# State-space heads computed with channels in the partitions instead of positions

## The reference, cut to what matters

```python
xbc = silu(causal_dwconv(xbc, conv_w, conv_b)); xs, bm, cm = split(xbc)
a_cs = cumsum(dt * a)                                   # per head
lmat = exp(where(causal, a_cs[l] - a_cs[s], -inf))      # decays between positions
y_diag = (cm @ bm.T * lmat) @ (xs * dt)                 # inside a chunk, per head
y_off  = (cm @ prev_state) * exp(a_cs)                  # what the first chunk leaves to the second
y = y_diag + y_off + xs * d_skip
out = rmsnorm(y * silu(z)) * norm_g                     # z = h @ w_in[:, 0:1024]
```

## Time and profile before

| | us |
|---|---|
| median of 3 runs | 2436.69 (2436.45 to 2437.45) |
| the profiled execution's own time | 2437.16 |
| its span in the profile | 2435.3 |
| PE busy | 2427.0 |
| PEld busy | 2022.1 |
| DVE busy | 1965.2 |
| ACT busy | 1263.7 |
| POOL busy | 106.7 |

### The profile page before, as it was taken

The page is one execution under the profiler, slowest core; times in us unless marked ns, Lnnn a source line. Parts: engine busy times, 40 slices in busy tenths (PEclk is TensorE's granted clock), DMA queues, the critical chain, the costliest instruction groups (busy, mean ns, idle before and its releaser), DMA issues.

```text
span 2435.3 us, 30633 instructions
## 1 busy us (share of the span) xinstructions
PE 2427.0 (100%) x11686; PEld 2022.1 (83%) x11686; DVE 1965.2 (81%) x3206; ACT 1263.7 (52%) x1680; POOL 106.7 (4%) x128
## 2 busy tenths in 40 slices
PE   9999999999999999999999999999999999999999
PEld 7888888888888888888888888888888888888887
DVE  8787978888888788888767798878878867797877
ACT  5445654454456544544556655544544557664543
POOL 0000000000000000000100020000000100020000
PEclk9999999999999999999999999999999999999999
DMA  8775455656754566676564564565666644555663
GB/s 259 236 242 169 158 188 192 193 186 196 238 179 156 176 197 197 205 231 209 176 197 139 175 215 156 191 196 181 209 193 201 200 162 153 173 203 167 200 194 122
DMA packets 325905, 463.35 MB, mean 190 GB/s; under 512 B 18608, under 2 KB 237056, under 8 KB 325504
## 3 DMA queue, kind: packets, MB, share of 16 engines
q1 hardware_dynamic: 321792, 452.90, 57.3%
q10 hardware_dynamic: 3968, 8.49, 1.2%
HBM read 457.11 MB, written 4.23 MB: 189 GB/s over the span
## 4 chain that ended last, share of the span: by engine, by line
PE 98%; DVE 1%; DMA 1%; SPq 0%; ACT 0%; issue 0%; DVEq 0%; ACTq 0%
PE acc L733 47%; PE work L733 38%; PE acc L947 4%; PE acc L950 2%; PE work L1002 1%; PE acc L1039 1%; DMA raw<-ffn_w_dram 1%; PE work L740 1%; PE work L1020 1%; PE work L768 1%; DVE w_lo L1860 0%; PE acc L1280 0%; PE work L1190 0%; PE acc L1279 0%; PE acc L768 0%; PE work L1076 0%
## 5 line engine op out<-in xcount | busy, mean ns | idle before, releaser
L1860 DVE TENSOR_TENSOR w_lo<-raw,w_hi 128x2048 fp32r<-128x2048 f32 x416 | 947.7, 2283 | 214.3 <-ACT w_hi L1327 210.9
L1327 ACT CAST w_hi<-raw 128x2048 fp32r<-128x2048 f32 x416 | 789.2, 1903 | 292.1 <-PE acc L733 93.1
L733 PE MATMUL work<-w_hi,xt_both 128*128 128x512 f32 x2784 | 872.6, 389 | 0.8 <-DVE field L1964 0.8
L733 PEld LDWEIGHTS work<-w_hi,xt_both 128*128 128x128 f32 x2784 | 522.6, 188 | 110.5 <-issue 1.6
L733 PE MATMUL work<-w_lo,xt_both 128*128 128x512 f32 x1392 | 541.6, 389 | 0.0
L733 PE MATMUL acc<-w_hi,yt_hi 128*128 128x512 f32 x1088 | 427.1, 393 | 0.0
L733 PE MATMUL acc<-w_hi,yt_lo 128*128 128x512 f32 x1088 | 423.8, 389 | 0.0
L733 PE MATMUL acc<-w_lo,yt_hi 128*128 128x512 f32 x1088 | 423.4, 389 | 0.0
L2037 DVE STREAM_TRANSPOSE field<-field 32x128 f32<-32x128 f32 x1280 | 387.7, 303 | 19.1
L733 PE MATMUL acc<-w_hi,xt_both 128*128 128x512 f32 (+2 forms) x1280 | 393.9, 384 | 0.0
L733 PEld LDWEIGHTS work<-w_lo,xt_both 128*128 128x128 f32 x1392 | 261.3, 188 | 54.0
(11 more groups left out here) (210 smaller groups left out, 1600.7 us busy)
## 6 DMA issues: line engine op xcount, KB each, us to landing
raw<-ffn_w_dram SPq DMA_DIRECT2D x260, 512.0 KB, 4.6
raw<-w_in_dram SPq DMA_DIRECT2D x208, 512.0 KB, 4.5
raw<-w_ffn_in_dram SPq DMA_DIRECT2D x176, 512.0 KB, 4.7
raw<-w_ffn_out_dram SPq DMA_DIRECT2D x88, 512.0 KB, 4.3
raw<-w_branch_dram SPq DMA_DIRECT2D x48, 512.0 KB, 4.5
raw<-w_out_dram SPq DMA_DIRECT2D x32, 512.0 KB, 4.3
bias<-b_gate_dram SPq DMA_DIRECT2D x10, 512.0 KB, 5.6
raw<-w_branch_pool_dram SPq DMA_DIRECT2D x8, 512.0 KB, 4.3
```

What stands on the lines that cost most here:

```text
L733: last = nc.tensor.matmul(out, x[:, kt, k], y, start=start and n == 0, stop=stop and n == 2)
L1327: nc.scalar.copy(w_hi[:, slot, 0:n], raw[:, at, 0:n]).then_inc(hi_split[slot], 1)
L1860: nc.vector.tensor_tensor(w_lo[:, at, 0:n], raw[:, at, 0:n], w_hi[:, slot, 0:n].bitcast(F32), ALU.subtract).then_inc(unit_split[slot], 1)
```

## The change

- z is projected turned (`z_turned`): a 128x128 block of weight is stationary and 256 positions move, 192 matmuls in place of 96. DVE scales the result by the row factor as it reads it (`z_scaled`), ACT takes the silu in place (`z_silu`). The four z units are loaded as 256 columns by 8 row tiles instead of 512 by 4.
- The heads are computed turned, in four batches of four: a 128x64 block of `xdt` (or of `scaled`, what the first chunk carries over) is stationary, the masked decays (128 positions) move, two heads go to the two column halves of the array. The carried part is a third product per head that accumulates in PSUM, so `carried`, `carry` and the middle block's separate decay go. The decays after the first chunk are kept in two versions, `after` and the new `late`; POOL makes them with 32 instructions of 128x128.
- The skip part is one DVE instruction per 128x256 tile with d_skip per partition; the second product of `rows_xs` goes.
- The gated result is already turned: the 16 transposes go, ACT and DVE split it from SBUF. For the norm the sum runs over partitions: ACT squares, POOL adds the eight tiles (1024, 512 and 256 columns), PE multiplies by a column of -1 (`sqs`), DVE scales.
- `spread_sums(3)` is issued one z step earlier.

```diff
@@ SP
-                chunks("w_in_2", 0, 2)
+                for c in range(4):
+                    load(next(at), whole("w_in_2", l, 0, 256 * c, 256, 8))
@@ POOL
-                                nc.gpsimd.tensor_tensor(after[:, hd, :, :], after[:, hd, :, :],
-                                                        starts[:, :, hd:hd + 1].broadcast_to([P, 2, P]), ALU.subtract) \
+                                nc.gpsimd.tensor_tensor(after[:, hd, 0, :], after[:, hd, 0, :],
+                                                        starts[:, 0, hd:hd + 1].broadcast_to([P, P]), ALU.subtract) \
                                     .then_inc(after_ready, 1)
+                            pool.wait_ge(conv_ready, 3 * l + 3)
+                            for hd in range(16):
+                                nc.gpsimd.tensor_tensor(S["late"][:, hd, :], after[:, hd, 1, :],
+                                                        starts[:, 1, hd:hd + 1].broadcast_to([P, P]), ALU.subtract) \
+                                    .then_inc(late_ready, 1)
+                            pool.wait_ge(y_squared, 4 * l + 4)
+                            for k, n in enumerate((4, 2, 1)):
...
+                                nc.gpsimd.tensor_tensor(S["squares"][:, 0:n, :], S["squares"][:, 0:n, :],
+                                                        S["squares"][:, n:2 * n, :], ALU.add).then_inc(y_summed, 1)
@@ PE
-                chunk("z", 0, 40)
+                def z_turned(c, q):
...
+                    for j in range(2):
+                        out = acc[2 * pair + q][:, j * 256:(j + 1) * 256]
+                        for kt in range(kd):
...
+                            nc.tensor.matmul(out, hi, xt_hi[:, kt, :], start=kt == 0, stop=False)
+                            nc.tensor.matmul(out, hi, xt_lo[:, kt, :], start=False, stop=False)
+                            last = nc.tensor.matmul(out, lo, xt_hi[:, kt, :], start=False, stop=kt == kd - 1)
-                    nc.tensor.matmul(acc[2 * pair][:, c:c + 64], w[:, 0:P], S["xdt"][:, 0, v], start=True, stop=True)
-                    nc.tensor.matmul(acc[2 * pair + 1][:, c:c + 64], w[:, P:2 * P], S["xdt"][:, 1, v], start=True,
-                                     stop=True).then_inc(y_done, 1)
+                def heads(i):
+                    g = i // 2
+                    pair, n = count("chunks", 1, l, "ys", g)
+                    pe.wait_ge(chunk_read[pair], n * 2 - 1 + i % 2)
+                    pe.wait_ge(scaled_ready, 2 * l + g + 1)
+                    pe.wait_ge(seg_ready, 4 * l + i + 1)
+                    for t in range(2):
...
+                        for s in range(2):
+                            nc.tensor.matmul(out[s][:, early], S["xdt"][:, 0, v[s]], after[:, hds[s], 0, :],
+                                             start=True, stop=True)
+                        for s in range(2):
+                            nc.tensor.matmul(out[s][:, late], S["scaled"][g][:, hds[s] % 8 * 64:hds[s] % 8 * 64 + 64],
+                                             after[:, hds[s], 1, :], start=True, stop=False)
+                        for s in range(2):
+                            last = nc.tensor.matmul(out[s][:, late], S["xdt"][:, 1, v[s]], S["late"][:, hds[s], :],
+                                                    start=False, stop=True)
+                    last.then_inc(y_done, 1)
                 half("gate_s", 0, 0, 44, 0)
                 half("gate_s", 0, 0, 44, 1)
-                carried()
-                heads(range(0, 3))
+                heads(0)
                 half("gate_s", 0, 1, 44, 0)
-                heads(range(3, 6))
+                heads(1)
                 half("gate_s", 0, 1, 44, 1)
-                heads(range(6, 8))
                 half("gate_s", 1, 0, 46, 0)
-                heads(range(8, 11))
+                heads(2)
                 half("gate_s", 1, 0, 46, 1)
-                heads(range(11, 16))
+                heads(3)
                 half("gate_s", 1, 1, 46, 0)
-                turn(1, l, "turn_s", S["y"], range(4), lambda i: pe.wait_ge(y_ready, 2 * l + (1 + i // 2)))
                 half("gate_s", 1, 1, 46, 1)
-                chunk("br_s", 0, 48, yt, "turn_s")
+                both("br_s", 0, 0, 48, yt, "y")
+                both("br_s", 0, 1, 48, yt, "y")
+                bank, filled = fill(1, l, "sqs")
+                pe.wait_ge(y_summed, 3 * l + 3)
+                for r in range(2):
+                    last = nc.tensor.matmul(bank[:, r:r + 1], S["squares"][:, 0, r * P:(r + 1) * P], minus_one[:, 0:1],
+                                            start=True, stop=True)
@@ ACT: through(45) / z_silu(0, 0), z_silu(0, 1) / through(46) / z_silu(1, 0), z_silu(1, 1) / factors
+                def decays(i):
+                    hds = slice(BATCH * i, BATCH * (i + 1))
...
+                    nc.scalar.activation(x, x, ACT.Relu, scale=-1.0)
+                    nc.scalar.activation(y, y, ACT.Relu, scale=-1.0).then_inc(exponents_bounded, 1)
+                    act.wait_ge(exponents_bounded, 4 * l + i + 1)
+                    nc.scalar.activation(x, x, ACT.Exp, scale=-1.0)
+                    nc.scalar.activation(y, y, ACT.Exp, scale=-1.0).then_inc(decay_ready, 1)
                 decays(0)
                 through(47)
                 decays(1)
                 decays(2)
                 through(48)
                 decays(3)
-                decays(4)
@@ DVE, around rows_xs and the heads
+                z_scaled(1, 0)
                 through(45)
+                z_scaled(1, 1)
                 rows_xs(1)
...
+                def weights(i):
+                    dve.wait_ge(decay_ready, 4 * l + i + 1)
+                    x = after[:, BATCH * i:BATCH * (i + 1), :, :].rearrange("p h r q -> p h (r q)")
+                    tt(x, x, S["cb"][:, i // 2, 0:2 * P].unsqueeze(1).broadcast_to([P, BATCH, 2 * P]), ALU.mult)
+                    x = S["late"][:, BATCH * i:BATCH * (i + 1), :]
+                    tt(x, x, S["cb"][:, i // 2, 2 * P:3 * P].unsqueeze(1).broadcast_to([P, BATCH, P]), ALU.mult) \
+                        .then_inc(seg_ready, 1)
+                def outputs(i):
...
+                    for t in range(2):
+                        y = S["y"][:, 2 * i + t, :]
+                        last = stt(y, y, vec[:, 100 + 2 * i + t:101 + 2 * i + t],
+                                   acc[2 * pair + i % 2][:, t * 256:(t + 1) * 256], ALU.mult, ALU.add)
+                    last.then_inc(chunk_read[pair], 1)
...
+                    tt(y, y, S["z"][:, 2 * i:2 * i + 2, :], ALU.mult).then_inc(y_ready, 1)
+                scale_early(0)
+                weights(0)
                 through(47)
+                weights(1)
+                scale_early(1)
                 through(48)
                 add_bias(1, l, "gate_s", 0, m + 45, S["gate"][:, :, 0:512], 0, 0, (0,))
+                weights(2)
                 add_bias(1, l, "gate_s", 0, m + 45, S["gate"][:, :, 0:512], 0, 0, (1,))
+                outputs(0)
+                outputs(1)
+                weights(3)
                 through(49)
+                outputs(2)
+                outputs(3)
                 through(50)
+                for i in range(4):
+                    dve.wait_ge(y_hi, 4 * l + i + 1)
...
+                        last = stt(yt_lo[:, t, :], S["y"][:, t, :], vec[:, gain("s") + t:gain("s") + t + 1],
+                                   yt_hi[:, t, :].bitcast(F32), ALU.mult, ALU.subtract)
+                    last.then_inc(y_split, 1)
```

More of the change, by code:

```diff
@@ L104, in tables @@
         norms=Table(1, [norms]),
-        squares=Table(1, [[u for u in norms if not u[0][2].startswith("post_")]]),
+        squares=Table(1, [[u for u in norms if u[0][2].startswith("pre_") or u[0][2] == "final"]]),
         means=Table(1, [[u for u in norms if not u[0][2].startswith("pre_")]]),
@@ L932, in part @@
                     if turn_name and r == 0 and kt % 2 == 0:
-                        turned(block, l, turn_name, kt // 2)
+                        if name == "br_s":
+                            pe.wait_ge(y_split, 4 * l + kt // 2 + 1)
+                        else:
+                            turned(block, l, turn_name, kt // 2)
                     last = product(x[0], x[1], kt, r, pos, t * cols, cols, acc[2 * pair + r][:, 0:cols],
@@ L1283, in heads @@
-                def heads(hds):
-                    for hd in hds:
-                        weigh(hd)
+                def heads(i):
[5 more added lines that the diff above has]
+                    for t in range(2):
+                        hds = [BATCH * i + 2 * t + s for s in range(2)]
+                        early, late = (slice(t * 256 + r * P, t * 256 + (r + 1) * P) for r in range(2))
+                        out = [acc[2 * pair + i % 2][64 * s:64 * s + 64, :] for s in range(2)]
+                        v = [slice(hd * 64, hd * 64 + 64) for hd in hds]
+                        for s in range(2):
[8 more added lines that the diff above has]
```

(58 more changed lines are left out.)

119 lines of the change are left out of this document (66 added, 53 removed).

## The result

The changed kernel takes 2443.4 us (2443.18 to 2444.47, 8 runs) against 2436.57 (2435.72 to 2438.35, 8 runs): ratio 1.0028, 95% interval 1.0019 to 1.0038. The forecast was 2440.6, inside a range of 2432 to 2446.5. The profiled execution has a span of 2441.6, where the kernel before had 2435.3.

The account below looks back on a forecast made before the run. PE was taken to bound the kernel, with DVE at 94%. Waits of 5.5 per layer against 3.1 saved; br_s start and sqs gave +1.95 per layer: 2437.16 + 3.9 - 0.47 = 2440.6 us, range 2432 to 2446.5.

Parts of the forecast that it names:

- PE's work: PE's matmuls and transposes, removed against added: 3.1 us less per layer, 6.2 in all, if PE never waits.
- The sum of squares: Two added PE matmuls of 4 records for the norm: +0.45 us per layer, between 0.2 and 0.9.
- A batch: Four heads on PE in column halves, 12 matmuls or 24 records: 1.48 us each, four adding 5.94 per layer.
- rival D: Each change of tiling mode costs a full drain on the waiting path: at most +2.6 us, 2443.2; chance 0.05.
- PE's waits: PE waits for the ACT and DVE chain that feeds the heads: 5.5 us per layer, against 3.1 saved.
- heads(0): PE reaches the first batch at 1462.6, DVE's weights(0) are done at 1463.75: waits 1.15 us.
- unit 46, first half: Its PSUM is released by DVE's bias, behind the split that waits for ACT's cast 48: PE waits 1.85 us.
- br_s, first pair: br_s needs yt_lo, whose first pair DVE finishes at 1490.2; PE arrives at 1489.0: waits 1.2 us.
- the lows: DVE's instructions writing yt_lo before br_s: the first pair was taken as 0.80 us.
- rival C: POOL is late: at 1.41 us per late subtraction the clamps wait, +5 in all, 2445.6; late squares add 2; chance 0.15.
- A: The forecast itself: PE waits of about 4 to 7 us per layer, 2437.5 to 2443.5; chance 0.55.
- B: Waits are shorter and PE's work decides: 2430.5, or about 2434 with a third of the waits left; chance 0.25.

Follow-up runs that it names:

- h6: e1's kernel with the decays' exponentials (ACT) and the products with cb (DVE) left out, so not the reference's result: 2431.71 us.
- h9: e4 with PE's first two batches of heads directly behind one another, after unit 45's second half: 2432.73 us, ratio 0.9985 to the kernel before.
- e2: The changed kernel with ACT's cast of unit 48 moved ahead of the third batch of decays: 2436.1 us.
- e3: The changed kernel with ACT's clamps of batches 0 and 1 moved ahead of the silu of z's last quarter: 2437.74 us.
- e1: The changed kernel with POOL's sum of squares held back until DVE has written all of yt_lo: 2441.13 us.
- e4: The changed kernel with the edits of e1, e2 and e3 together: 2433.68 us, ratio 0.9989 to the kernel before.
- g7: e4 with DVE's split of unit 46 moved ahead of z's last scaling: 2435.93 us, ratio 0.9997 to the kernel before.

## Why the prediction held, step by step

**PE's work.** Predicted -3.1 per layer, measured -2.48 (h6). z is 0.12 per matmul, as predicted; from its first matmul to `cb` it takes 24.75 (1430.59 to 1455.34) where it took 23.58 (1430.99 to 1454.57), +1.17 and not +1.28. The sum of squares is 0.92 - 0.45 = 0.47 (predicted 0.45). A batch is 1.67, not 1.48: the mis-sized term. Four batches make +0.75, z takes 0.11 off, and the sum comes to -2.46. That is rival D's mechanism: the prediction asked whether four changes more than the earlier trace rows price in cost 0.65, and by h9 four changes, two pairs, cost 2 x 0.32 = 0.64. The rule of the Trainium skill, TensorEngine Tiling (Array Packing), Key Properties, that a change of mode drains TensorE, agrees with this trace, and 0.16 per change is also what a matmul's modelled length exceeds its distance by.

**PE's waits.** Predicted 5.5 per layer, measured 6.03, but put together otherwise:

| wait | predicted | measured, with the 0.16 |
|---|---|---|
| heads(0) | 1.15 | 1.40 |
| heads(1) | 0.7 | 0.56 |
| unit 46, first half | 1.85 | 1.59 |
| heads(2) | 0.6 | 0.31 |
| br_s, first pair | 1.2 | 0.78 |
| br_s, second pair | none | 1.37 |

The mechanism of the first five is the one given, with the releasers given: z ended at 1455.34 (predicted 1455.85), the first clamp started at 1458.35 (1458.85), cast 48 at 1469.39 (1469.95), the bias ended at 1474.26 (1474.7). The four common rows are early by about 0.5 because z itself began 0.4 earlier than before and cost 0.1 less than forecast. e2 and e3 show that the chain through ACT's list is the cause of the waits before br_s's second pair and not only beside them.

**The step that was missing: the lows.** The prediction took 0.80 for a pair of lows from the earlier trace rows, and saw POOL's sum of squares only as something that could itself be late. It wasn't (done at 1494.58, asked for at 1502.27), but it doubled the lows' time. The page of the Trainium skill cited for rival C, GPSIMD Engine Reference, Specifications, names the condition: DVE instructions with two SBUF inputs. The lows read PSUM in the earlier trace rows (`work`) and SBUF after the change (`field`), so the change itself brought them under that rule; e1 agrees, 6.90 beside POOL against 3.25 without. No run has lows that read PSUM beside POOL; the nearest is the bias pair in e1, which reads PSUM and wasn't slowed. The prediction applied it to POOL's time and, but for 0.4 on one split, not to DVE's.

**The sum.** -2.48 + 6.03 = +3.55 per layer. The prediction's own terms, -3.1 + 5.5, make +2.4; it gave +1.95 from the schedule's start of br_s, 0.45 less than its terms, and didn't notice. So of the miss of 1.6 per layer 0.45 is that slip, 0.6 PE's work, 0.5 the waits. These three are why the forecast of 2440.6 was low by 2.8. The mechanism was right, but the size was not: the loss is 6.8 where 3.9 was forecast, and 2443.4 lies 0.1 inside the end of A's own range. All three errors have the same sign. That D's 2443.2 is the nearest figure is luck: D reached it from mode changes alone, at +2.6, and they gave about half of that.

**The rivals.** B (PE's work decides) needed waits below 3.1 per layer and had 6; e4 and h9 show that its region could be reached by order alone. C was wrong in its first part: the late subtractions take 7.82 / 16 = 0.49 on average, not 1.41, and ACT's clamp waits for none in the changed kernel. Its mechanism was real all the same: a subtraction that starts inside a DVE split is held up once, to the split's end, whatever its width, but only one is held per split (the first of the 16 takes 2.44, the next ones 0.36 each). That is what g7 ran into, once e3's order had taken the slack away. The prediction read the 1.41 of the earlier trace rows as the price of every subtraction beside DVE; it is a mean over eight, of which the two that start inside a split take 2.66 each and those beside instructions that read PSUM 0.61. C's second part, the squares late, didn't happen either.

## What to carry to other kernels

Work removed from a full PE counts only if the engines that feed it keep their dates: here 2.5 us per layer were removed and 6.0 of waits came, and moving one cast up by one item in ACT's list took 4.05 of them out. Look for the engine that idles ahead of the first wait, and move what it waits for, before judging a change by its time; with three reorderings the same change went from 0.28% slower to 0.11% faster. When an operand moves from PSUM to SBUF, price the instruction again for whatever POOL does beside it, and look at which of the two starts first, instruction by instruction: a mean over a group hides that one was held and the others weren't.

## What the runs showed of the hardware

- A group of matmuls with 64-column stationary blocks between ordinary ones costs a pair of changes of 0.32 us (h9 against e4). Going from f32r to plain f32 and back with the whole array costs nothing that shows (three and five heads of the kernel before, 1.35 and 2.24).
- Between a POOL instruction and a DVE instruction with two SBUF inputs, the one that started first kept its time and the other ended only behind it. POOL held a low of 0.48 for 2.61 (changed kernel) and a split of 2.27 for 3.46 (e1). A split held POOL's addition of 512 columns for 3.23 (e1; 1.35 beside the lows) and its 128x128 subtraction for 2.44 (g7). In e2 a low that started 0.04 ahead of POOL was not held.
- Where DVE doesn't hold it, POOL's subtraction takes 0.61 with 256 columns (kernel before) and 0.40 with 128 (h9, 0.36 from start to start), so halving the columns doesn't halve it. The 0.74 of the earlier trace rows was not undisturbed: in it most take 0.80, beside DVE's convolution.
